# Identity products on TensorE in the waits of the routings and ahead of two combines

## The reference

```python
probs = softmax(xt @ w_router + b_router)
best_group = argmax(sum of the top 2 probs of each group of 4)
vals, idx = top_k(where(in_group, probs, -1), 2);  gates = vals / vals.sum(-1)
for e in range(16):
    h = silu(xt @ w_gate[e]) * (xt @ w_up[e])
    y = y + dense_gate[:, e:e+1] * (h @ w_down[e])
x = layer_norm(ALPHA * x + y)
```

## Time and profile before

| | us |
|---|---|
| median of 3 runs | 1638.11 |
| lowest, highest | 1632.55, 1643.83 |
| span of the profiled execution, first to last instruction | 1637.2 |
| TensorE busy | 1449.6 (89%) |
| VectorE busy | 642.2 (39%) |
| ScalarE busy | 366.8 (22%) |
| GpSimd busy | 207.0 (13%) |
| mean granted clock of TensorE | 0.927 |

### The profile page before, as it was taken

How to read it: one execution, slowest core, us unless ns; L and a number is a source line. 1 busy time by engine, 2 the same in 40 slices (tenths; PEclk the granted TensorE clock), 3 DMA queues, 4 the chain that set the end, 5 groups by cost and what they waited for, 6 DMA issues and landing times. The chain is left out here.

```text
span 1637.2 us, 26246 instructions
## 1 busy us (share of the span) xinstructions
PE 1449.6 (89%) x10111; PEld 889.8 (54%) x10112; DVE 642.2 (39%) x1022; ACT 366.8 (22%) x789; POOL 207.0 (13%) x266
## 2 busy tenths in 40 slices
PE   6999999966779998999749999994994699999968
PEld 4566666645668895445424444443794344444423
DVE  1122553069245562867551111115795211111117
ACT  1333110066523332111201111111231111111111
POOL 4000000000054332110001101005000101010040
PEclk9999999988689999999959999996797799999989
DMA  6673110041020003000378796776005688786353
GB/s 194 133 284 132 29 26 26 0 115 22 9 51 4 4 4 114 28 26 27 114 261 298 261 332 235 271 240 245 1 28 202 235 270 303 277 281 223 146 217 120
DMA packets 137055, 236.96 MB, mean 145 GB/s; under 512 B 20178, under 2 KB 100035, under 8 KB 136682
## 3 DMA queue, kind: packets, MB, share of 16 engines
q1 hardware_dynamic: 113458, 151.01, 29.0%
q0 software_dynamic: 16880, 60.49, 10.0%
q10 hardware_dynamic: 6624, 24.12, 3.7%
HBM read 178.92 MB, written 58.21 MB: 145 GB/s over the span
## 5 line engine op out<-in xcount | busy, mean ns | idle before, releaser
L2299 PE MATMUL ex_pb<-ew_w_gate_up,ex_xT 128*128 x736 | 330.0, 602 | 6.0 <-issue 3.7
L298 PE MATMUL pj_pb<-pj_xT,pj_w 128*128 128x348 f32 (+3 forms) x960 | 282.1, 455 | 0.8 <-ACT pj_xT L322 0.8
L298 PEld LDWEIGHTS pj_pb<-pj_xT,pj_w 128*128 128x128 f32 (+1 forms) x960 | 178.8, 186 | 101.9 <-ACT pj_xT L322 0.8
L2299 PEld LDWEIGHTS ex_pb<-ew_w_gate_up,ex_xT 128*128 128x128 f32 x736 | 138.0, 192 | 165.2 <-issue 164.1
L2282 PE MATMUL ex_pb<-ew_w_down,ex_hiddenT 128*128 x368 | 165.7, 593 | 3.4 <-ACT ex_hiddenT L2369 3.4
L2492 DVE TENSOR_TENSOR ex_hidden<-ex_hidden,ex_pb 128x256 f32<-128x256 f32 x46 | 19.4, 421 | 324.6 <-ACT ex_hidden L2364 324.6
L2282 PEld LDWEIGHTS ex_pb<-ew_w_down,ex_hiddenT 128*128 128x128 f32 x368 | 66.3, 190 | 69.9 <-issue 69.9
L2487 DVE COPY ex_y_rows<-ex_pb 128x512 f32<-128x512 f32 x46 | 31.8, 692 | 134.5 <-PE ex_pb L2282 134.5
L430 DVE SCALAR_TENSOR_TENSOR mixed<-pj_pb,v_mu,mixed 128x347 f32<-128x347 f32 (+3 forms) x42 | 24.0, 572 | 145.7 <-ACT mixed L372 145.6
L2364 ACT ACTIVATE ex_hidden<-ex_pb 128x256 f32<-128x256 f32 x46 | 17.7, 386 | 261.4 <-PE ex_pb L2299 261.4
L2242 POOL COPY ex_tokens_now<-ex_token_of_slot 128x1 uint32 (+1 forms) x48 | 9.6, 200 | 451.3 <-PE ex_pb L2271 399.3
(11 more groups left out here) (423 smaller groups left out, 2061.2 us busy)
## 6 DMA issues: line engine op xcount, KB each, us to landing
ew_w_gate_up<-in_w_ex_gate SPq DMA_DIRECT2D x32, 1024.0 KB, 8.4
ew_w_gate_up<-in_w_ex_up SPq DMA_DIRECT2D x32, 1024.0 KB, 11.0
ew_w_down<-in_w_ex_down SPq DMA_DIRECT2D x32, 1024.0 KB, 13.1
scratch_slots_out<-ex_y_rows ACTq DMA_DIRECT2D x46, 512.0 KB
scratch_slots_out<-pj_tmp POOLq DMA_DIRECT2D x4, 4096.0 KB, 16.0
scratch_x_stored<-x_rows SPq DMA_DIRECT2D x16, 512.0 KB
pj_w<-in_w_in SPq DMA_DIRECT2D x7, 1024.0 KB, 10.5
minus_kk_then_y<-in_x_prompt SPq DMA_DIRECT2D x8, 512.0 KB
```

What stands on the lines that cost most here:

```text
L298: last = nc.tensor.matmul(product(at)[:, 0:tn], w[:, s % NW, k, c0:c0 + mrows], xT[:, k, x0:x0 + tn], start=(k == 0), stop=(k == KD - 1))
L2299: last = mm(pb[:, 2 + u, :], xT[:, u, k, :], w[:, k, :], start=(k == 0), stop=(k == KD - 1))
```

## The change

A new function multiplies the 128x128 identity by itself a number of times, into the first 128 columns of a PSUM bank. The results are not read. It is called in five places of the source, of which the three in the experts' stage are run for both layers: 28 products before the wait for the assigned experts, 28 behind the counts, 24 behind the token list; 60 at the start of the first combine, 32 at the start of the last. These are 252 products more in a run.

```diff
+def keep_busy(nc, bank, ident, times):
+    for _ in range(times):
+        nc.tensor.matmul(bank[:, 0:P], ident[:, :], ident[:, :], start=True, stop=True)
@@ combine_pool_mix @@
         @block.tensor
         def _(pe):
             mm = nc.tensor.matmul
+            keep_busy(nc, pb[:, 7, :], const["ident"], 60)
             pe.wait_ge(pm.sem, pm.all)
@@ experts @@
             a = A[:, :, :].rearrange("p t e -> p (t e)")
+            keep_busy(nc, pb[:, 1, :], const["ident"], 28)
             pe.wait_ge(tables.sem, tables.all)
             pe.wait_ge(r["as"], 1)
             mm(pb[:, 5, 0:TILES * E], t["ones"][:, :], A[:, :, :].rearrange("p t e -> p e t"), start=True, stop=True)
             mm(pb[:, 6, 0:TILES * E], t["not_earlier"][:, :], a, start=True, stop=True).then_inc(r["rk"], 1)
+            keep_busy(nc, pb[:, 1, :], const["ident"], 28)
             pe.wait_ge(r["blocks"], 1)
...
             mm(pb[:, 4, 0:NBLK], part, group_sum[:, :], start=True, stop=True).then_inc(r["tokens"], 1)
+            keep_busy(nc, pb[:, 2, :], const["ident"], 24)
             transpose_x(0, 0)
@@ combine @@
         @block.tensor
         def _(pe):
+            keep_busy(nc, pb[:, 7, :], const["ident"], 32)
             pe.wait_ge(q["alpha"], 1)
```

## The result

The changed kernel takes 1647.4 us (median of 9 runs, 1641.31 to 1653.95) against 1638.11 of the kernel before (9 runs, 1631.82 to 1644.89). The ratio is 1.0048, 95% interval 1.0025 to 1.0072: half a per cent slower, outside the range of 1615 to 1641. The profiled execution took 1641.38 us, 6 under its median, with a span of 1639.6. So its trace shows only a part of the loss: by the spans 2.4 us, by the medians 9.3.

What follows compares the result with a forecast made beforehand. TensorE was taken to bound the expert stages, its slow clock after waits costing time. Routings 12.3 won, less 1.5, plus 1.4 and 0.2 in the combines, made 12.4 us, from 1637.2 to 1624.8, said as 1626 us; range 1615 to 1641.

Steps and rivals of the forecast that it cites:

- net 0.2 won: Last combine: the 32 end 2.5 us late, the cold 5.25 us become 2.57; from 0.8 lost to 1.0 won.
- nothing else pays: All five places: added products use unused PSUM, touch no semaphore, DMA or queue, so cost nothing elsewhere.
- The price of an added product and the rise of the clock: All five places: 0.465 us each at half clock, 0.233 at full, which comes after 4.4 us of products.
- Rival 3: All five places: the identity times itself doesn't raise the clock, each product costs 0.465 us; 1685 us, chance 0.09.
- The routings: Both layers' routings and first expert groups: 5.75 and 6.5 us won, together 12.3, less 1.5 for a falling clock.
- rival 4: Ahead of the first expert groups: transposes let the clock fall, 2.05 and 2.78 us lost; 1631 us, chance 0.05.
- My allowance of 1.5 us: One of two routings: the clock falls in the narrow token products between the second 28 and the 24.
- 1.4 won: First combine: the 60 end 0.7 us late at 16.2, sample pooling takes 6.3 instead of 8.4; 3.5 won to 2.4 lost.
- Rival 2: First combine: the clock stays up through TensorE's 25.00 us from 1140 to 1165; 1617 us, chance 0.09.
- the sign that I had named for being wrong: Changed kernel's profile: added products at 0.465 us to their end, or a clock of 1.00 between 1140 and 1165.
- the bound of 8.7: First combine, 1140 to 1165: at most 8.7 us won, since VectorE is busy for 16.32 of the 25.00.
- Slower than before: Whole kernel: slower by more than about 1 per cent (16 us), chance 0.10, Rival 3 included.

Runs made afterwards that it cites:

- e2: The kernel before plus only the 32 added products of the last combine; 1652.59 us, ratio 1.0084.
- e1: The changed kernel without the 60 and the 32, so only the routings' added products remain; 1631.4 us against 1637.24, ratio 0.9956.
- h1: g4 without the 4 wide products of the last combine, so nothing is added there; 1624.01 us, ratio 0.9933.
- g3: The changed kernel with nothing added in the first combine and 4 products of 512 columns in place of the 32; 1630.36 us, ratio 0.9952.
- g4: g3 plus 15 products of 512 columns in the first combine, in place of the 60; 1623.48 us, ratio 0.9914.
- e3: The kernel before plus, in the last combine only, 8 products of 512 columns in place of the 32; 1641.66 us, ratio 1.0027.
- g1: e2 with the last combine's gather held until the 32nd added product is done; 1648.98 us, ratio 1.0074.
- g2: e2 with 16 added products in place of 32; 1644.71 us, ratio 1.0040.
- e4: The kernel before plus only the 60 added products of the first combine; 1636.0 us, ratio 0.9988.
- h2: e4 with the first combine's gather held until the 60th added product is done; one execution, 1642.36 us (before: 1639.09).

## Why the prediction was wrong, step by step

**The failed step: the last combine, "net 0.2 won", and with it "nothing else pays: ... they wait on no semaphore and set none, and no DMA, no queue of SyncE or GpSimd is touched".** That sentence looks only at what an instruction waits for and sets. The 32 products did share something with the gather that ran beside them, and TensorE's next signals came 11.5 us late. Measured in this stage: 12.2 us lost (76.6 against 64.4), of which 11.0 lie between 15.2 and 26.2 us, the points at which VectorE began on tile 0 before and in the changed kernel. On tile 0's records 0.6 us were won, near the forecast 0.2. By the medians the 32 alone cost 15.3 us (e2). Without this step the kernel gains: e1 has 5.8 us by the medians, h1 15.1.

The trace of before held a warning that I did not read. VectorE's timeline, last combine of the kernel before:

```profile
1588.04 1.30 DVE L1730 BATCH_NORM_STATS2 cb_stats<-cb_pb 128x6 f32<-128x512 f32 x2 [19.46 <-issue]
...
1595.64 1.30 DVE L1730 BATCH_NORM_STATS2 cb_stats<-cb_pb 128x6 f32<-128x512 f32 x2 [2.87 <-issue]
```

Tile 1's records end 20.3 us after the start (1593.07), but VectorE begins at 1595.64, 2.6 us later, idle for 2.87 with no cause named. TensorE's signals ran late beside the gather already. I had read this stage only up to the first product, where the change is.

**The price of an added product and the rise of the clock: right.** 28 products took 8.33 us (forecast 8.7), the next 28 6.41 (6.5), the 24 5.60 (5.6), the 32 9.31 (9.6). This is TensorE's timeline in layer 0's routing; to be held against the earlier trace rows:

```profile
819.08 8.33 PE L141 MATMUL ex_pb<-k_ident 128*128 128x128 f32 x56 [1.18 <-PEq L119]
828.73 0.71 PE L2326 MATMUL ex_pb<-ex_assigned,rt_ones 128*128 128x144 f32 x2 [1.31 <-DVE ex_assigned L2439]
829.26 0.42 PE L2327 MATMUL ex_pb<-ex_assigned,rt_not_earlier 128*128 128x144 f32 x2
829.52 6.41 PE L141 MATMUL ex_pb<-k_ident 128*128 128x128 f32 x56
837.52 1.18 PE L2335 MATMUL ex_pb<-ex_xT,ex_x_rows 128*32 128x128 f32 x18 [1.59 <-DVE ex_xT L2474]
838.70 1.18 PE L2335 MATMUL ex_pb<-ex_y_rows,ex_x_rows 128*32 128x128 f32 x18
...
840.54 5.60 PE L141 MATMUL ex_pb<-k_ident 128*128 128x128 f32 x48
847.02 1.09 PE L2280 MATMUL ex_pb<-k_ident,ex_x_rows 128*128 128x128 f32 x8 [0.88 <-DMA ex_x_rows<-scratch_x_stored,ex_tokens_now]
849.70 8.83 PE L2308 MATMUL ex_pb<-ew_w_gate_up,ex_xT 128*128 x16 [1.59 <-DVE ex_xT L2356]
```

Rival 3, that the identity doesn't raise the clock, is refuted by the first row: 0.30 us a product, not 0.465.

**The routings: right in kind, 10.8 forecast, 8.5 measured.** The pieces shrank nearly as forecast: the counts to 0.95 (829.68 - 828.73; forecast 0.7), the token groups to 1.18 each, the transposes to 1.09. From the stage's start to that of the first expert group 2.7 and 2.95 us were won in the two layers, where the pieces of the forecast add up to 3.7 in each. The large miss is the last row: 8.83 us where 7.03 was forecast. The clock fell in layer 0 under the transposes or in the wait behind them, which is rival 4 in one layer of two; in layer 1 and in both layers of e1 the group takes 7.13, but in e1's layer 0 it is the following block's that takes 8.83. My allowance of 1.5 us was for a fall among the token products, which happened in g3 (1.9 us up to the first expert group of layer 1) and not here; the fall that happened here cost 1.8. So the size was near, the place was not. "TensorE: Matmul & The Clock Gate", Part 4, of the Trainium skill says that transposes do not count as a busy TensorE in the way that products do. The row of 8.83 can be read so, but the fall can't be told from one in the wait behind them, and in g3 the first expert group of layer 0 took 7.13 us behind the same transposes; those of the earlier trace rows stand against the rule.

**The first combine: "1.4 won" was right for a stream without holes, and the 60 had holes.** They ended 20.9 us after the stage's start, not 16.2. The pooling ended 3.0 us later than before, and its signal reached ScalarE late as well (1142.11, with the last records ended at 1139.68). So with the 60 the next tile's products start 31.3 us after the stage's start, 5.4 later than before: this term was wrong by 6.8 us, for the same reason as the last combine. With 15 wide products instead, g4, the next tile starts 1.46 us earlier than before, the forecast figure. Rival 2, which I gave 0.09, is what happened in addition, with the sign that I had named for being wrong, full clock between 1140 and 1165. The same window as in the earlier trace rows, shifted to where TensorE works again, in the changed kernel:

```profile
1146.00:1165.00 19.00, 17.52 (x101) 11.88 (x100) 15.69 (x22) 5.09 (x8) 0.00 (x0) 0.97 0.00 1
```

0.97 instead of 0.50, and it gave the stage what the 60 had lost and 3.0 us more. In g4 9.9 - 1.5 = 8.4 us came this way, against the bound of 8.7 that VectorE's busy time had set. I held it for unlikely because 8-column work does not hold the clock. That is so (in g4 the pooling falls to half pace after 2 us). But the clock came back under the next tile's eight products with 128 columns, 28 us after the stage's start in g4 and about 34 with the 60, 2.9 to 3.5 us after these eight began; in g3, where nothing was added, just behind them, at 30; and before only at about 51. It then stayed up under the products with 8 rows and 256 columns that follow. Of the kernels with nothing added here, six (before, e1, e2, e3, g1, g2) have 138.2 to 139.2 us and one, g3, 133.7; the four with added products beside the gather have 129.3 to 136.2. That the wide ones help is borne out by 129.3 and 129.4 and by the medians (g4 6.9 us under g3); by which rule the clock comes back is open, and so is how often it does so with nothing added, since each kernel has one trace.

**The chances.** Slower than before had 0.10, from a price of the product and from two mishaps added up. None of my rivals let an added product slow the work of another engine. The sum without the failed step, 1626, is where g4 and h1 are (1623.5, 1624.0), but partly by rival 2 and so not a confirmation.

## What to carry to other kernels

Filler work on TensorE was not free here just because TensorE was idle. If a GpSimd gather is in flight, count the filler's instructions, take few and wide ones (512 columns instead of 128 for the same microseconds), and look at when the *next* engine starts, not at TensorE's own rows. Where an engine begins some microseconds behind the last record that it needs, with "issue", "remote" or a transfer long landed as the cause, signals may be late there already; here more small instructions made that worse (2.6 us before at tile 1, 8.3 with 16 products). And read a stage to its end even when the change stands at its beginning.

## What the hardware showed that I had not expected

- TensorE's completion signals can be late while a gather by GpSimd is in flight: 11.5 us at the first tile with 64 records ahead of it (e2, the changed kernel 11.7); at the second tile 8.3 us with 32 (g2), 3.5 with 16 (e3), 2.4 to 3.3 with 8 (g3, g4), and with none 2.6 (before) or 0.1 and less (e1, e4, h1, h2). In the two worst kernels and in g2 they come in at about 26 us after the stage's start, when the gather's traffic ends (26.5 to 28.5 us). Held apart, both work undisturbed (g1: 0.11 us; h2: no holes).
- It isn't DMA traffic as such. In layer 0's routing of the changed kernel 112 added records ran without a hole (56 from 819.08, 56 from 829.52), and the products behind them followed their tables, while the weights' transfers, issued by SyncE, had all DMA engines busy from 822 on. The window of the second 56:

```profile
829.50:836.00 6.50, 6.43 (x58) 6.24 (x56) 5.69 (x18) 0.00 (x0) 0.00 (x0) 1.00 1.10 357
```

- What the two share is not settled. Each product of float32 leaves two records of work, and whether it is the products, their loads of weights, the semaphores' path or the writing of the records itself that backs up behind the gather's descriptors, these runs don't separate. The last can't be ruled out, because each of these executions has its span and clock from such records; whether a kernel timed without them loses the 12 us is open. The Trainium skill, "NOTIFIC — Programmer's Manual", section 1.2, says that such records are written to rings in memory and that a queue whose ring is full can be set to stall the engine that produces them; no run here shows whether that takes part.
- Products of the identity with 128 columns take about 0.43 us at half clock and 0.22 at full (two records each, from the starts of the records); 15 with 512 columns took 15.1 us.
- Products with 8 rows and 512 columns don't always hold the clock: in the samples' tile of the last combine it fell to 0.50 in e1 and stayed at 1.00 in e2, behind the same kind of products.
